# Block one of a transformer pair as a single stage: recurrence products placed between projection products, outputs token-major

## The chip, the cores and the metric

One core of one Trainium2 chip. The time is the device time of one launch in microseconds (us). The kernel before was run three times: 2466.53 us (median), 2466.32 us (lowest), 2470.12 us (highest).

## The reference

All arithmetic is float32. Block one takes 512 tokens `x` and 256 context tokens of width 1024 (8 tiles of 128 columns). Cut to what the change touches:

```
mod_x, mod_c = silu(c) @ w_ada + b_ada, silu(c_ctx) @ w_ada + b_ada   # six parts of 1024
p = modulate(rmsnorm(h), shift, scale) @ w_in      # 512 q,k | 512 v | 512 g | 32 r | 512 pool
gk_f, gk_b = log_sigmoid(r_f @ w_gk_f + b) / 16, log_sigmoid(r_b @ w_gk_b + b) / 16
# chunks of 64 positions, 4 heads, 64 keys x 128 values, forward and backward
u     = einsum(k * exp(b_last - bcum), v);  S[n+1] = exp(b_last) * S[n] + u[n]
a     = tril(einsum(q * exp(bcum - b_mid), k * exp(b_mid - bcum)))
o     = a @ v + (q * exp(bcum)) @ S[n]             # summed over both directions
mix   = concat(o * rsqrt(mean(o*o) + eps) * w_norm * silu(g),
               pool_project(window means of pool_in over 2,4,8,16 minus the token))
h     = x + g1 * (mix @ w_out)
```

The context's chunks only advance the state; they have no outputs. Then come a mixture of experts (32 experts, 4 for each token) and a second block. Neither is touched.

## The kernel before, in words

The kernel writes the order of work of each engine by hand; engines wait for each other through semaphores. Block one is five phases, each a block of its own, so that an engine begins a phase only when all engines have finished the one before.

- **phase_in (L147).** The sync engine loads `x`, the context, and then weight tiles of 2 MB into a ring of six slots in the order of `Weights` (L76 to L85): four tiles of `w_ada`, then parts of `w_in` and the other eight tiles of `w_ada`. TensorE makes modulation rows (`ada`, L260), spreads them (L271, L274), turns the tokens feature-major (L281) and makes 20 projection products (`project`, L297): 18 with 512 moving columns and two with 256, eight matmuls each. Four banks rotate; odd products are copied out by ScalarE (L231), even ones by VectorE (L417, L419). GpSimd issues 15 transfers of zeros for the experts' output (L249). The pooled features come last.
- **phase_gates (L491).** TensorE makes the gate inputs (L527); ScalarE takes them out and makes Abs, Exp and Ln (L537 to L542); VectorE takes the minimum, scales, scans four rows of 768 and subtracts (L565, L566, L569, L574, L579); ScalarE exponentiates (L545 to L553); VectorE multiplies with q and k (L584 to L589). q is spread over zeroed 128-row tiles `qmid` and `qcum`, so a score or an output of one head contracts over 128 rows of which 64 are zero. GpSimd makes window sums of two of four pooling groups (L765 to L781).
- **phase_gla (L592).** 24 transposes of the decayed keys (L632), 11 steps of the recurrence (L643 on TensorE, four updates on VectorE at L705), scores for four token tiles (L654) masked by VectorE (L714, L718), then outputs head by head and feature-major (L663, L668; 16 and 64 matmuls), their squares (L688), means over 128 features by a matmul with a tile of 1/128 (L677), a square root and a reciprocal over 2048 columns (L690, L725), norm and gate (L728, L730). GpSimd makes the other two pooling groups.
- **phase_pool (L784).** Four products with `w_pool` (L794), scaled (L801).
- **phase_out (L805).** `x` is read again (L817), 8 products with `w_out` (L826), gated and added (L840, L842).

Then the routing phase of the experts begins with its DMAs (L997, L1017) and squares (L1021).

Of the kernel before, what the change touches and what calls it, by code (L numbers as in the profile page):

```python
# [21 lines left out]
P = 128  # L22
# [29 lines left out]
ADA_FIRST = (0, 2, 1, 3)  # L52
ADA_REST = [("ada2", [6, 7]), ("ada3", [8, 9]), ("ada4", [4, 5, 10, 11])]
# [4 lines left out]
class Weights:  # L58


    def __init__(self, nc, top, k, a):
# [12 lines left out]
        ada = lambda tiles: cols(a["w_ada"], [(i * 512, 512) for i in tiles])  # L74
        win = lambda name: cols(a["w_in"], [W_IN[name]])
        add("ada1", *ada(ADA_FIRST))  # L76
        add("in_r", *win("r"))
        add("in_qk", *win("qk"))
        add("in_v", *win("v"))
        add(ADA_REST[0][0], *ada(ADA_REST[0][1]))  # L80
        add("in_g", *win("g"))
        add(ADA_REST[1][0], *ada(ADA_REST[1][1]))
        add("in_pool", *win("pool"))
        add(ADA_REST[2][0], *ada(ADA_REST[2][1]))
        add("out", *cols(a["w_out"], [(0, 512), (512, 512)]))  # L85
        self.before_moe = len(self.jobs)
# [5 lines left out]
        self.slot = [n % SLOTS if n < self.first["out2"] else (n - self.first["out2"]) % SLOTS for n in range(len(self.jobs))]  # L92
# [54 lines left out]
def phase_in(nc, k, a, w, xt, hT, g):  # L147

    ps = k.ps
    ADA1, R, QK, V, G, PL = (w.first[n] for n in ("ada1", "in_r", "in_qk", "in_v", "in_g", "in_pool"))  # L150
    columns = list(ADA_FIRST)
    tiles = [ADA1 + i for i in range(4)]
    for name, cols in ADA_REST:
        tiles += [w.first[name] + i for i in range(len(cols))]
        columns += cols
    with ExitStack() as st:
        sem = lambda n: k.semaphore(n)
        sb = lambda n, s, d=F32: st.enter_context(nc.sbuf_tensor(n, s, d))
        rows, rows2 = sb("vec_rows", [2 * KD, P]), sb("vec_rows_2", [P, P])
        brows, bcol = sb("b_ada_rows", [48, P]), sb("b_ada_cols", [P, 48])  # L160
        bg = sb("b_ada_gates", [P, 2, D])
        sig = sb("sigmoid_c", [P, 2 * KD])
        narrow = sb("silu_narrow", [P, KD, 32])
        modr = sb("mod_rows", [P, 2, P])
        pick = sb("pick_row", [P, 4, P])
        junk, ms, rt = sb("sq_junk", [P, D]), sb("ms", [P, NT]), sb("rt", [P, NT])
        zero = sb("y_zero", [P, D])
        c_in, vec_in, vec_in_2, bg_in, const_in = (sem(n) for n in ("c_in", "vec_in", "vec_in_2", "bg_in", "const_in"))
        x_in = [sem(f"x_in_{i}") for i in range(NT)]
        c_turn, c_cols, sig_done, narrow_done, v_turn, v_cols, v_zero = (sem(n) for n in ("c_turn", "c_cols", "sig_done", "narrow_done", "v_turn", "v_cols", "v_zero"))  # L170
        sq, msd, sd, xnd, x_turn, x_out, vch, modx = (sem(n) for n in ("sq", "mean_sq", "sd", "xn_done", "x_turn", "x_out", "vch", "modulated"))
        mm, rowd, picked, turn, cold, halfd = (sem(n) for n in ("ada_mm", "ada_rows", "pick_ready", "ada_turn", "ada_cols", "mod_half"))
        r_mm, r_out, pj, ev_v, ev_a = (sem(n) for n in ("r_mm", "r_out", "proj_mm", "proj_ev_v", "proj_ev_a"))
        zd, zero_out = sem("y_zero"), sem("y_zero_out")
        block = st.enter_context(nc.Block())

        jobs = []

        def feat(n, col, dst, lo, nn, post=None):
            jobs.append((n, lambda kk: w.tile(n)[:, kk, col:col + P], lambda kk: hT[:, kk, lo:lo + nn], nn, dst, post))  # L180

        for m in range(2):
            feat(QK, m * P, g.qT[:, m, :], 0, T, 64.0 ** -0.5)
        for m in range(2):
            feat(QK, 256 + m * P, g.kT[:, m, 0:T], 0, T)
            feat(QK, 256 + m * P, g.kT[:, m, T:TC], T, CTX)
        for i in range(NT):
            jobs.append((V, lambda kk, i=i: hT[:, kk, i * P:(i + 1) * P], lambda kk: w.tile(V)[:, kk, :], 512, g.v[:, i, :], None))
        for m in range(4):
            feat(G, m * P, g.gT[:, m, :], 0, T)  # L190
        for m in range(4):
            feat(PL, m * P, g.poolT[:, m, :], 0, T)

        def gate(t):
            return columns[t] // 2 in (2, 5)

        @block.sync
        def _(sp):
            for i in range(NT):
                src = a["x"][0, i * P:(i + 1) * P, :] if i < TT else a["ctx"][0, (i - TT) * P:(i - TT + 1) * P, :]  # L200
                sp.dma_start(xt[i], src).then_inc(x_in[i], 16)
            w.load(sp, 0, w.before_moe)

        @block.scalar
        def _(act):
            for name, r in VEC_LIST[0:2]:
                act.dma_start(rows[VEC[name]:VEC[name] + r, :], a["vec_views"][name]).then_inc(c_in, 16)
# [6 lines left out]
            act.dma_start(k.ones128[:], a["const_ones128"]).then_inc(const_in, 16)  # L214
            for i in range(NT):
                act.wait_ge(x_in[i], 16)
                act.activation(junk[:], xt[i], ACT.Square, accum_out=ms[:, i:i + 1]).then_inc(sq, 1)
                act.wait_ge(sq, i + 1)
            act.wait_ge(msd, 1)
            act.activation(rt[:], ms[:], ACT.Sqrt).then_inc(sd, 1)  # L220
            for i in range(NT):
                for h in range(2):
                    act.wait_ge(x_turn, 2 * i + h + 1)
                    act.activation(hT[:, 4 * h:4 * h + 4, i * P:(i + 1) * P], ps[2 * (i % 2) + h][:].rearrange("p (q t) -> p q t", q=4), ACT.Copy).then_inc(x_out, 1)
            for i, gi in enumerate((2, 5)):
                act.dma_start(bg[:, i, :], a["b_ada"][0:1, gi * D:(gi + 1) * D].to_broadcast([P, D])).then_inc(bg_in, 16)
            act.wait_ge(const_in, 16)
            for j in range(1, len(jobs), 2):
                n, lhs, rhs, nn, dst, post = jobs[j]
                act.wait_ge(pj, j + 1)  # L230
                act.activation(dst, ps[j % 4][:, 0:nn], ACT.Copy, scale=1.0 if post is None else post).then_inc(ev_a, 1)  # L231

        @block.gpsimd
        def _(pool):
            for name, r in VEC_LIST[3::2]:
                pool.dma_start(rows2[VEC[name]:VEC[name] + r, :], a["vec_views"][name]).then_inc(vec_in_2, 16)
            pool.memset(pick[:], 0.0).then_inc(picked, 1)
            for q in range(4):
                pool.wait_ge(picked, q + 1)
                pool.memset(pick[32 * q:32 * q + 1, q, :], 1.0).then_inc(picked, 1)  # L240
            pool.wait_ge(picked, 5)
            pool.memset(zero[:], 0.0).then_inc(zd, 1)
            pool.wait_ge(zd, 1)

            pool.wait_ge(pj, 6)
            first = 2 * E_ * SUB
            n = (MAX_SUBS * SUB - first) // P
            for i in range(n):
                pool.dma_start(k.y[first + i * P:first + (i + 1) * P, :], zero[:]).then_inc(zero_out, 16)  # L249
            pool.wait_ge(zero_out, 16 * n)  # L250

        @block.tensor
        def _(pe):
            def ada(t):
                w.wait(pe, tiles[t])
                if t >= 2:
                    pe.wait_ge(rowd, t - 1)
                for kk in range(KD):
                    for q in range(4):
                        last = pe.matmul(ps[4 + t % 2][32 * q:32 * q + 32, 0:P], narrow[:, kk, :], w.tile(tiles[t])[:, kk, q * P:(q + 1) * P], start=kk == 0, stop=kk == KD - 1)  # L260
                last.then_inc(mm, 1)

            def spread(t):
                pe.wait_ge(rowd, t + 1)
                if t >= 2:
                    pe.wait_ge(cold, t - 1)
                bank = ps[6 + t % 2]
                if gate(t):
                    pe.wait_ge(picked, 5)
                    for q in range(4):  # L270
                        last = pe.matmul(bank[:, q * P:(q + 1) * P], pick[:, q, :], modr[:, t % 2, :], start=True, stop=True)  # L271
# [4 lines left out]
            def turn_x(i):  # L276
# [3 lines left out]
                for kk in range(KD):  # L280
                    last = pe.transpose(ps[2 * (i % 2) + kk // 4][:, (kk % 4) * P:(kk % 4 + 1) * P], xt[i][:, kk * P:(kk + 1) * P], k.ident[:])  # L281
# [3 lines left out]
            def used():  # L285
                pe.sem_inc(w.used, 1)

            def project(lo, hi):
                for j in range(lo, hi):
                    n, lhs, rhs, nn, dst, post = jobs[j]  # L290
                    w.wait(pe, n)
                    if j >= 4:
                        pe.wait_ge(ev_v if j % 2 == 0 else ev_a, (j - 4) // 2 + 1)
                    for kk in range(KD):
                        if j == 0:
                            pe.wait_ge(modx, 2 * kk + 2)
                        last = pe.matmul(ps[j % 4][:, 0:nn], lhs(kk), rhs(kk), start=kk == 0, stop=kk == KD - 1)  # L297
                    last.then_inc(pj, 1)
# [24 lines left out]
            pe.wait_ge(mm, 4)  # L323
            for _ in range(4):
                used()

            project(0, 1)
            w.wait(pe, R)
            pe.wait_ge(rowd, 4)
            for kk in range(KD):  # L330
                for q in range(4):
                    last = pe.matmul(ps[4][32 * q:32 * q + 32, 0:192], w.tile(R)[:, kk, :], hT[:, kk, 192 * q:192 * q + 192], start=kk == 0, stop=kk == KD - 1)
            last.then_inc(r_mm, 1)
            pe.wait_ge(r_mm, 1)
            used()
            project(1, 6)
            pe.wait_ge(pj, 6)
            used()
# [2396 lines left out]
```

## Time and profile before

| what | value |
|---|---|
| time, median of 3 runs | 2466.53 us |
| time of the profiled execution | 2470.89 us |
| its span, first to last instruction | 2469.1 us |
| PE (matmul) busy | 2075.9 us, 84% |
| PEld (weight load) busy | 1019.4 us, 41% |
| VectorE (DVE) busy | 731.5 us, 30% |
| ScalarE (ACT) busy | 301.4 us, 12% |
| GpSimd (POOL) busy | 261.8 us, 11% |
| HBM traffic over the span | 221 GB/s |
| mean granted TensorE clock | 0.906 of 2.4 GHz |

PE is TensorE's matmuls, PEld its weight loads, which overlap them. A busy share says that an engine had an instruction in flight, not that it bounds the time. PEclk is the granted clock as a share of 2.4 GHz: 1.00 is 2.4 GHz and 0.50 is 1.2 GHz. "Idle before" names how long an engine stood still before a group and which instruction released it. A float32 matmul has two records in the trace, a transpose one. Block one ends some 439 us into the span.

### The profile page before, as it was taken

To read this page: it belongs to the slowest core of one execution; us is meant where nothing else is said; L and a number is where in the kernel's file an instruction comes from. 1 tells how busy PE (TensorE), PEld (TensorE's weight loads), DVE (VectorE), ACT (ScalarE), POOL (GpSimd) and SP (SyncE) were. 2 spreads that over 40 slices of the span, in tenths; PEclk is the share of its full clock that TensorE was granted. 3 is DMA by queue.
4 is the path that set the end of the run, shared out by engine and by line. 5 is a ranking of instruction groups with operands and counts; after the bars stand their busy time and mean duration, and the time that the engine had idled before them with its cause. 6 is when DMAs were issued, how large, how long until landed. Compare 5 with 4: busy or idle time off the path is not lost. (4 is left out here: it accounts for less than half of the span.)

```text
span 2469.1 us, 41438 instructions
## 1 busy us (share of the span) xinstructions
PE 2075.9 (84%) x17351; PEld 1019.4 (41%) x17351; DVE 731.5 (30%) x1338; ACT 301.4 (12%) x567; POOL 261.8 (11%) x299
## 2 busy tenths in 40 slices
PE   6992368449987989999989895199998789999998
PEld 3442263314422434433424332144776444444443
DVE  2004742413322223222323221665645320110001
ACT  2002200300000000000000000233233110000001
POOL 1105420021100111111101011100320000000000
PEclk9997659679988999999989998599997899999999
DMA  9533000669999999999999999310101311222000
GB/s 369 206 137 126 3 0 34 262 255 410 414 419 419 417 419 419 417 418 418 418 419 418 415 417 376 129 35 0 36 23 35 145 68 68 98 72 77 34 0 34
DMA packets 132029, 548.44 MB, mean 222 GB/s; under 512 B 19610, under 2 KB 32942, under 8 KB 82514
## 3 DMA queue, kind: packets, MB, share of 16 engines
q1 hardware_dynamic: 105936, 506.21, 50.9%
q0 software_dynamic: 9264, 27.04, 2.9%
q10 hardware_dynamic: 16690, 13.06, 1.7%
q8 instruction: 120, 1.97, 0.3%
q14 instruction: 19, 0.16, 0.0%
HBM read 523.54 MB, written 22.71 MB: 221 GB/s over the span
## 5 line engine op out<-in xcount | busy, mean ns | idle before, releaser
L1244 PE MATMUL ps<-W,x_modulated 128*32 128x512 f32 x3168 | 381.7, 622 | 92.6 <-DVE x_modulated L1322 43.2
L1244 PE MATMUL ps<-W_high,x_modulated 128*32 128x512 f32 x2016 | 241.2, 617 | 26.2 <-DMA W_high<-in_w_gu 20.2
L1244 PEld LDWEIGHTS ps<-W,x_modulated 128*32 128x32 f32 x3168 | 107.9, 112 | 328.0 <-issue 189.8
L2624 PE MATMUL ps<-hT,W 128*128 128x512 f32 x512 | 224.3, 599 | 3.2 <-PE ps L2624 1.8
L2662 PE MATMUL ps<-W,hid 128*128 128x512 f32 x512 | 221.6, 593 | 2.7 <-PEq L2606 1.7
L1331 DVE TENSOR_SCALAR gate<-ps 128x256 f32<-128x256 f32 x81 | 34.4, 425 | 601.8 <-PE ps L1248 601.8
L1260 PE MATMUL ps<-W,hidden_turned 128*32 128x256 f32 x3200 | 186.4, 384 | 1.1 <-DVE hidden_turned L1342 1.1
L2624 PEld LDWEIGHTS ps<-hT,W 128*128 128x128 f32 x512 | 97.6, 192 | 129.5 <-issue 129.5
L2662 PEld LDWEIGHTS ps<-W,hid 128*128 128x128 f32 x512 | 96.6, 190 | 127.7 <-issue 127.7
L1260 PEld LDWEIGHTS ps<-W,hidden_turned 128*32 128x32 f32 x3200 | 118.3, 112 | 73.9 <-issue 21.8
L1642 PE MATMUL ps<-hT,W 128*128 128x512 f32 x336 | 146.5, 594 | 2.4 <-PEq L1437 2.1
L1244 PEld LDWEIGHTS ps<-W_high,x_modulated 128*32 128x32 f32 x2016 | 71.2, 111 | 170.4 <-issue 121.6
L1285 ACT ACTIVATE sig<-gate 128x256 f32<-128x256 f32 x81 | 33.8, 418 | 693.5 <-DVE gate L1331 693.5
L1260 PE MATMUL ps<-W_high,hidden_turned 128*32 128x256 f32 x1984 | 114.1, 381 | 0.0
L1215 POOL COPY rows_idx<-slot_rows 128x1 int32 (+1 forms) x82 | 22.7, 277 | 831.2 <-DVE x_turned L1318 825.9
L1642 PEld LDWEIGHTS ps<-hT,W 128*128 128x128 f32 x336 | 63.3, 190 | 82.2 <-issue 82.0
L297 PE MATMUL ps<-hT,W 128*128 128x512 f32 (+1 forms) x224 | 93.4, 577 | 2.2 <-DMA W<-in_w_in 2.0
L1260 PEld LDWEIGHTS ps<-W_high,hidden_turned 128*32 128x32 f32 x1984 | 70.0, 111 | 46.6 <-issue 11.9
L1218 POOL DMA_INDIRECT x_rows<-moe_xn,rows_idx x82 | 80.4, 981 | 64.6 <-POOL rows_idx L1215 64.6
L2642 DVE TENSOR_TENSOR hid<-relu_tmp 128x512 f32<-128x512 f32 x32 | 22.2, 693 | 205.9 <-ACT relu_tmp L2636 205.9
L2562 PE MATMUL ps<-W,mixT 128*128 128x512 f32 x128 | 57.4, 607 | 14.0 <-PEq L1997 13.9
L1342 DVE STREAM_TRANSPOSE hidden_turned<-hidden 128x256 f32<-128x256 f32 x81 | 36.1, 446 | 110.0 <-ACT y_rows L1292 110.0
(541 smaller groups left out, 2036.0 us busy)
## 6 DMA issues: line engine op xcount, KB each, us to landing
W<-in_w_gu SPq DMA_DIRECT2D x152, 1024.0 KB, 25.4
W_high<-in_w_gu SPq DMA_DIRECT2D x104, 1024.0 KB
W<-in_w_down SPq DMA_DIRECT2D x80, 1024.0 KB, 23.5
W_high<-in_w_down SPq DMA_DIRECT2D x48, 1024.0 KB
W<-in_mlp_w SPq DMA_DIRECT2D x16, 2048.0 KB, 7.8
W<-in_w_ada SPq DMA_DIRECT2D x12, 2048.0 KB, 15.4
W<-in_w_in SPq DMA_DIRECT2D x10, 2048.0 KB, 16.8
moe_y<-y_rows ACTq DMA_DIRECT2D x324, 32.0 KB, 5.9
```

The costliest lines, as they stand in the source:

```text
L297: last = pe.matmul(ps[j % 4][:, 0:nn], lhs(kk), rhs(kk), start=kk == 0, stop=kk == KD - 1)
L1215: pool.tensor_copy(rows_idx[:], m.idx4[:, bass.ds(u, 1)]).then_inc(idx_set, 1)
L1218: pool.indirect_dma_start(xg[:], None, m.xn, bass.IndirectOffsetOnAxis(ap=rows_idx[:, 0:1], axis=0)).then_inc(x_in, 16)
L1244: last = pe.matmul(gu_out(j), xs[:, kk, :], quarter(ex.view(n), j), start=kk == 0, stop=False)
L1260: last = pe.matmul(down_bank[SUB * j:SUB * (j + 1), 0:256], hT[:, kk, :], ex.view(n)[:, kk % 2, j * 256:(j + 1) * 256], start=kk == 0, sto ...
L1285: act.activation(sig[:], gate[:], ACT.Sigmoid, scale=1.702).then_inc(sigd, 1)
L1331: dve.tensor_scalar(gate[:], gu_bank[:, 0:256], SWIGLU_LIMIT, None, ALU.min).then_inc(gated, 1)
L1342: dve.transpose(hT[:].rearrange("p k t -> p (k t)"), hid[:]).then_inc(h_ready, 1)
L1642: last = pe.matmul(ps[j % 4][:, 0:nn], lhs(kk), rhs(kk), start=kk == 0, stop=kk == KD - 1)
L2562: last = pe.matmul(ps[2 * i + half][:], mixT[:, kk, i * P:(i + 1) * P], w.tile(O2 + half)[:, kk, :], start=kk == 0, stop=kk == KD - 1)
L2624: last = pe.matmul(ps[j % 8][:], w.tile(n)[:, kk, (j % 4) * P:(j % 4 + 1) * P], hT[:, kk, :], start=kk == 0, stop=kk == KD - 1)
L2662: last = pe.matmul(ps[2 * i + half][:], hid[:, 4 * g + q, i * P:(i + 1) * P], w.tile(L + g)[:, q, half * 512:(half + 1) * 512], start=g == ...
```

## The change

The five phases become one, `phase_first`. The rest of the kernel keeps its work; the second block's weights keep their slots.

- **Projections.** The pooled features come first, then k, q, v and g; v and g in token tiles. Two banks rotate in place of four. Pooled features are copied out by VectorE; k, q and v by ScalarE, in order with its exponentials.
- **Gates.** Made after two projection products. The division by 16 moves into the scale of the exponentials, so one pass over 3072 columns goes. Eight of the bias additions go to VectorE. The scaled minimum is made for 768 columns at a time, with a wait for each.
- **Keys, recurrence, scores.** Transposes and recurrence steps stand between v products; the last seven steps and the scores stand inside the four g products. Scores contract over 64 rows (no zeroed `qmid`, `qcum`).
- **Outputs.** Token-major: for one token tile 4 matmuls with 128 rows and 16 with 64 rows, 128 moving columns. The mean of squares comes from ScalarE's accumulator in place of a product; the gate is `silu(g) * w_norm` made by VectorE and GpSimd ahead of time. Each finished tile is transposed back and goes into `out`. Output products go tile by tile, both halves of a tile together.
- **GpSimd.** The pooling groups each wait for their own eviction. Then it zeroes the state and mask tiles, which lie in the same memory. The 15 transfers of zeros go to the sync engine's queue, in pieces of 1 KB in place of 4 KB.
- **Loads.** Weight tiles have fixed homes; a load waits for the product that frees its home. The reload of `x` waits for the last output.

TensorE's order after the opening (which stays):

```diff
+            pe.wait_ge(pool_in, 16)
+            project(0)
+            ...  (the r product)
+            project(1)
+            gates(0)
+            project(2)
+            gates(1)
+            ada(4)
+            project(3)
+            spread(4)
+            project(4)
+            ada(5)
+            project(5)
+            project(6)
+            spread(5)
+            ada(6)
+            project(7)
+            project(8)
+            spread(6)
+            ada(7)
+            project(9)
+            spread(7)
+            project(10)
+            project(11)
+            pe.wait_ge(feat, 2)
+            turn_k(0)
+            turn_k(1)
+            project(12)
+            pe.wait_ge(kdone, 2)
+            update(0)
+            project(13)
+            update(1)
+            turn_k(2)
+            turn_k(3)
+            project(14)
+            update(2)
+            project(15)
+            update(3)
+            turn_k(4)
+            turn_k(5)
+            ada(8)
+            for i in range(TT):
+                project(PROJ_G + i, 0, 3)
+                update(4 + 2 * i if i < 3 else 10)
+                project(PROJ_G + i, 3, 6)
+                if i < 3:
+                    update(5 + 2 * i)
+                scores(i)
+                project(PROJ_G + i, 6, KD)
+                spread(8 + i)
+                if i < 3:
+                    ada(9 + i)
+            pooled(0); pooled(1); outputs(0); pooled(2); pooled(3); outputs(1)
+            turn_mix(0); outputs(2); turn_mix(1); outputs(3)
+            out(0); turn_mix(2); out(1); turn_mix(3); out(2); out(3)
```

The rule by which a product waits for its bank, and ScalarE's order around the exponentials:

```diff
+            def project(j, lo=0, hi=KD):
+                    if 2 <= j < 6:
+                        pe.wait_ge(ev_v, j - 1)
+                    elif 6 <= j < 18:
+                        pe.wait_ge(ev_a, j - 5)
+                    elif j >= 18:
+                        pe.wait_ge(gmul, j - 17)
...
+            evict(4, k_out[0])
+            evict(5, k_out[1])
+            act.wait_ge(dl, 4)
+            act.activation(el, el, ACT.Exp, scale=1.0 / 16.0).then_inc(ee, 1)
+            evict(6, k_out[2])
+            act.wait_ge(dm, 4)
+            act.activation(ei, em, ACT.Exp, scale=-1.0 / 16.0).then_inc(ee, 1)
+            act.wait_ge(ee, 2)
+            act.activation(em, em, ACT.Exp, scale=1.0 / 16.0).then_inc(ee, 1)
+            evict(7, k_out[3])
```

The sync engine's order after the first four `w_ada` tiles:

```diff
+            sp.dma_start(w_r[:], ...); sp.dma_start(w_pool_in, ...); sp.dma_start(inv, ...); sp.dma_start(wp[:], ...)
+            sp.wait_ge(mm, 1)
+            load(0, w_ada(4))
+            sp.wait_ge(mm, 2)
+            load(1, w_cols(a["w_in"], *W_IN["qk"]))
+            ...  (v in two halves)
+            sp.wait_ge(mm, 3)
+            load(2, w_cols(a["w_in"], *W_IN["g"]))
+            for t in range(5, 9):
+                sp.wait_ge(mm, t)
+                load(0, w_ada(t))
+            for i in range(fills):
+                sp.dma_start(k.y[...].rearrange("p (q n) -> p q n", q=4), zero[...].to_broadcast([P, 4, 256])).then_inc(zero_out, 16)
+            sp.wait_ge(pj, PROJ_V)
+            load(1, w_cols(a["w_out"], 0, 512))
+            for t in range(9, 12):
+                sp.wait_ge(mm, t)
+                load(0, w_ada(t))
+                ...  (its bias row, after cold t)
+            sp.wait_ge(pj, PROJ_END)
+            load(2, w_cols(a["w_out"], 512, 512))
+            sp.wait_ge(o, TT)
+            ...  (x again, four transfers)
```

`mm` counts `ada` products, `pj` projections, `ev_v` and `ev_a` evictions by VectorE and ScalarE, `dl` and `dm` the subtractions, `feat` the products with q and k, `o` the outputs.

## Rows read from the trace of the kernel before

**Rows 1.** Busy time by stretch: us, busy by engine, granted clock, DMA share, GB/s.

```profile
42.10:204.60 162.50, 157.06 (x932) 81.32 (x932) 13.99 (x33) 5.55 (x10) 7.94 (x15) 0.98 0.57 211
204.60:278.00 73.40, 2.95 (x33) 2.47 (x33) 46.47 (x31) 25.77 (x28) 31.10 (x20) 0.55 0.09 31
278.00:313.90 35.90, 25.10 (x264) 20.02 (x264) 24.71 (x59) 6.78 (x8) 34.29 (x23) 0.79 0.02 5
313.90:348.10 34.20, 34.16 (x160) 34.16 (x161) 4.48 (x1) 1.79 (x3) 8.20 (x4) 0.50 0.00 0
348.10:382.10 34.00, 10.81 (x19) 4.04 (x18) 24.23 (x17) 3.79 (x3) 0.00 (x0) 0.65 0.00 0
382.10:437.70 55.60, 55.41 (x128) 24.12 (x128) 9.70 (x15) 0.00 (x0) 0.00 (x0) 1.00 0.11 38
```

**Rows 2.** TensorE in order of time: start, us, line, operation, idle before.

```profile
42.16 9.84 PE L297 MATMUL ps<-hT,W 128*128 128x512 f32 x16 [2.02 <-DMA W<-in_w_in]
51.92 2.81 PE L332 MATMUL ps<-hT,W 128*32 128x192 f32 x64
...
124.70 3.70 PE L260 MATMUL ps<-W,silu_narrow 128*32 128x128 f32 x128 [0.30 <-PE ps L297]
...
203.43 1.16 PE L271 MATMUL ps<-mod_rows,pick_row 128*128 128x128 f32 x8 [0.41 <-DVE mod_rows L381]
215.09 2.94 PE L527 MATMUL ps<-rT,wgk 32*128 32x192 f32 x32 [10.50 <-DMA wgk<-in_w_gk_b]
278.00 5.42 PE L632 MATMUL ps<-ident,elast 128*128 128x128 f32 x24 [59.96 <-PEq L497]
...
287.35 0.69 PE L643 MATMUL ps<-h,cum 64*64 64x128 f32 x16 [0.54 <-DVE S_ctx L705]
...
302.10 2.05 PE L654 MATMUL ps<-W 128*128 128x128 f32 x16 [1.52 <-DVE a_masked L714]
...
313.94 0.80 PE L663 MATMUL ps<-elast,h 128*128 128x128 f32 x2 [2.81 <-DVE elast L718]
...
375.55 5.25 PE L794 MATMUL ps<-poolT,w_pool_sb 128*128 128x512 f32 x8 [21.87 <-PEq L597]
...
409.95 27.70 PE L826 MATMUL ps<-W,mixT 128*128 128x512 f32 x64
```

**Rows 3.** ScalarE in order of time, in the gates stage and the opening.

```profile
9.37 0.19 ACT L217 ACTIVATION_READ_ACCUMULATOR sq_junk<-h 128x1 f32 x1
...
221.95 2.76 ACT L540 ACTIVATE W<-W 128x3072 f32<-128x3072 f32 x1
...
230.10 2.76 ACT L542 ACTIVATE W<-W 128x3072 f32<-128x3072 f32 x1
```

**Rows 4.** VectorE in order of time, the gates stage, the recurrence, the end.

```profile
232.97 3.94 DVE L565 SCALAR_TENSOR_TENSOR W<-W 128x3072 f32<-128x3072 f32 x1 [17.22 <-ACT W L542]
...
250.13 3.57 DVE L574 TENSOR_TENSOR elast<-cum 128x768 f32<-128x768 f32 x4
...
289.85 8.47 DVE L705 SCALAR_TENSOR_TENSOR W<-W,decay,ps 128x128 f32<-128x128 f32 x28
...
438.42 0.69 DVE L842 TENSOR_TENSOR h<-h,W 128x512 f32<-128x512 f32 x1
```

**Rows 5.** The scans' line: durations in ns, least, median, most.

```profile
L569 DVE TENSOR_TENSOR_SCAN cum<-scan_mask,W x4: 1726/2212/2748, 241.4 to 248.4; 128x768 f32<-128x768 f32 x4
```

**Rows 6.** GpSimd in order of time: transfers of zeros, additions of the second and third pooling group.

```profile
83.27 7.94 POOL L249 DMA_DIRECT2D moe_y<-y_zero  x15 [73.51 <-PE ps L297]
...
233.77 6.01 POOL L777 TENSOR_TENSOR pool_rows<-mixT 128x1344 f32<-128x1344 f32 x1
...
288.73 3.08 POOL L777 TENSOR_TENSOR pool_rows<-mixT 128x1344 f32<-128x1344 f32 x1
```

**Rows 7.** PE by stretch: us, busy, granted clock, DMA share, GB/s.

```profile
111.00:118.00 7.00, 7.00 (x18) 1.00 0.00 0
```

More of the change, by code:

```diff
@@ new lines, in phase_first, with state @@
+        tile = lambda i: slice(i * P, (i + 1) * P)
+        o_bank = lambda i: 6 if i % 2 == 0 else 4
+        out_bank = lambda i: 0 if i % 2 == 0 else 6
+        def state(d, step):
+            n = order[d][step] if step < NCH else None
+            if n is None or n >= XCH:
+                return S_ctx[:, step % 2, 2 * d:2 * d + 2, :]
+            return S[:, n, 2 * d:2 * d + 2, :]
+        jobs = [(lambda kk, m=m: w_pool_in[:, kk, tile(m)], lambda kk: hT[:, kk, 0:T], T) for m in range(4)]
@@ L240, in _ @@
                 pool.memset(pick[32 * q:32 * q + 1, q, :], 1.0).then_inc(picked, 1)
+            link = linker(pool, pch)
             pool.wait_ge(picked, 5)
[L242 to L249, printed above, removed]
@@ L270, in spread @@
                     for q in range(4):
-                        last = pe.matmul(bank[:, q * P:(q + 1) * P], pick[:, q, :], modr[:, t % 2, :], start=True, stop=True)
+                        last = pe.matmul(bank[:, tile(q)], pick[:, q, :], modr[:, t % 2, :], start=True, stop=True)
                     last.then_inc(turn, 1)
@@ new lines, in gates, with turn_k @@
+            def gates(d):
+                if d:
+                    pe.wait_ge(z_a, 1)
+                for m in range(2):
+                    for q in range(4):
+                        r = slice(32 * q, 32 * q + 32)
+                        last = pe.matmul(ps[4 + q][:, m * 192:m * 192 + 192], wgk[r, d, tile(m)], rT[r, :], start=True, stop=True)
+                last.then_inc(gk_mm, 1)
+            def turn_k(n):
+                i = STATE_TILES[n]
+                if n >= 2:
+                    pe.wait_ge(kdone, n - 1)
+                for q in range(4):
+                    last = pe.transpose(ps[4 + n % 2][:, tile(q)], el[:, q, tile(i)], k.ident[:])
+                last.then_inc(tr, 1)
@@ new lines, in update @@
+            def update(step):
+                if step:
+                    pe.wait_ge(sdone, 4 * step)
+                for d in range(2):
+                    n = order[d][step]
+                    r = halfs[n % 2]
+                    for h in range(4):
+                        at = (h // 2) * P
+                        last = pe.matmul(ps[6 + d][halfs[h % 2], at:at + P], el[r, 2 * d + h // 2, (n // 2) * P + 64 * (h % 2):(n // 2) * P + 64 * (h % 2) + 64],
+                                         v[r, n // 2, h * P:(h + 1) * P], start=True, stop=True)
+                last.then_inc(u, 1)
@@ L294, in project, with out @@
+            def out(i):
+                pe.wait_ge(mev, i + 1)
+                if i == 1:
+                    pe.wait_ge(mixed, 3)
+                for half in range(2):
+                    if i == 0:
+                        pe.wait_ge(slot_in[1 + half], 48)
+                    if i >= 2:
+                        pe.wait_ge(oev, 2 * (i - 2) + half + 1)
                     for kk in range(KD):
-                        if j == 0:
-                            pe.wait_ge(modx, 2 * kk + 2)
-                        last = pe.matmul(ps[j % 4][:, 0:nn], lhs(kk), rhs(kk), start=kk == 0, stop=kk == KD - 1)
@@ L298, in project @@
-                    last.then_inc(pj, 1)
+                        last = pe.matmul(ps[out_bank(i) + half][:], mixT[:, kk, tile(i)], slot[1 + half][:, kk, :], start=kk == 0, stop=kk == KD - 1)
+                    last.then_inc(omm, 1)
             pe.wait_ge(c_in, 48)
@@ L322, in _ @@
             spread(3)
[L323 to L329, printed above, removed]
+            pe.wait_ge(pool_in, 16)
+            project(0)
+            pe.wait_ge(r_in, 16)
             for kk in range(KD):
                 for q in range(4):
-                    last = pe.matmul(ps[4][32 * q:32 * q + 32, 0:192], w.tile(R)[:, kk, :], hT[:, kk, 192 * q:192 * q + 192], start=kk == 0, stop=kk == KD - 1)
+                    last = pe.matmul(ps[3][32 * q:32 * q + 32, 0:192], w_r[:, kk, :], hT[:, kk, 192 * q:192 * q + 192], start=kk == 0, stop=kk == KD - 1)
@@ L373, in _ @@
+            out(3)
         @block.vector
@@ L581, in _ @@
+            col(5)
+            row(6)
+            col(6)
+            dve.wait_ge(ev_a, 4)
             dve.wait_ge(ee, 6)
@@ new lines, in _ @@
+            dve.wait_ge(zeroed, 2)
+            dve.wait_ge(const_in, 32)
+            for step in range(4):
+                advance(step)
+            row(8)
+            for i in range(TT):
+                advance(4 + 2 * i if i < 3 else 10)
+                if i < 3:
+                    advance(5 + 2 * i)
+                mask(i)
+                gated(i)
+                col(8 + i)
+                if i < 3:
+                    row(9 + i)
+            dve.wait_ge(halfd, 4)
+            dve.wait_ge(cold, 12)
```

860 lines of the change are left out of this document (374 added, 486 removed).

## The prediction

> **What bounds the kernel now.** I read the busy time by stretch first. Up to 204.6 us TensorE works nearly without a gap at full clock; in the next 73.4 us it works 2.95 us, then 25.1 of 35.9, then 34.2 us at a granted clock of 0.50, then 10.8 of 34.0; the output projection fills 55.6 us at 1.00 [rows 1]. So from 204.6 to 382.1 us, 177.5 us, block one is a chain of elementwise stages with small matmuls between. The order of time shows why: TensorE stands 60.0 us for the gates phase to end and 21.9 us for the norm [rows 2]. Nothing is in flight to hide it, for each phase waits for all engines. DMA is idle too (shares 0.00 to 0.09), so no transfer bounds this part [rows 1]. The experts start after block one in both kernels; what block one saves, the kernel saves.
>
> **The sum, in TensorE's order.** The sum is made against the profiled execution (span 2469.1 us, own time 2470.9 us, 4.4 us over the median of the runs), in which block one's last VectorE instruction ends at 439.1 us [rows 4].
>
> *Opening.* Same work to 42.2 us, where the first projection waits for the fifth 2 MB tile [rows 2]; the pool columns take its place in the queue, behind the same bytes. Unchanged.
>
> *Projections and modulation, kept.* The first product took 9.84 us because the clock had to rise; 8 half products of the output projection took 27.7 us at full clock counted as four of 16 records each, 6.9 us a product [rows 2]. So 9.8 + 17 x 6.9 = 127.1, two of 256 columns at half of that 6.9, the r product 2.8, eight `ada` at 3.70 / 2 = 14.8, four spreads of a gate row at 1.16 and four single transposes at about 0.2: 5.4. Together 157.0 us.
>
> *Moved in.* Gate inputs: 2.94 us at a clock near 0.55, half of that at full clock; I take 1.5 (ends 1.5 and 2.9). Transposes of keys: 5.4 us at a low clock; I take 3.3 (ends 2.7 and 5.4). Eleven steps at 0.69 us: 7.6. Scores: 2.05 us a tile now, with 128 rows; the 64-row form is not in the trace. It has half the rows per matmul and the same columns, and is nearest to the recurrence row, 16 records of 64 rows in 0.69; I take 1.5 each, 6.0 (ends 2.8 and 8.2) [rows 1, 2]. Sum 18.4, and TensorE's dense part would end at 42.2 + 157.0 + 18.4 = 217.6 us.
>
> *Does the gate chain stay under the projections?* Gate inputs stand at about 70 us. Bias additions end near 73; Abs to the end of Ln took 10.9 us [rows 3]: 83.8. On VectorE a minimum over 3072 columns took 3.94, a scan 1.73 to 2.75, the subtraction 3.57 for four [rows 4, 5]. The short scans ran with GpSimd idle, the long ones beside its pooling, and a GpSimd addition that takes 3.08 alone took 6.01 there [rows 6]: the two slow each other. Now the whole chain runs beside pooling, so I take 1.0 to 1.2 for a minimum of 768, 2.5 for a scan and 5.4 for the subtractions: 83.8 + 4 x 3.8 + 0.3 + 5.4 = 104.8. ScalarE then exponentiates 3072 columns (2.8), and only behind that copies product 6 out: 108.2. Product 8 needs that bank and would be ready at 103.8. **Here is the wait that the change adds: 4.4 us**, ends 0 and 12. Queued behind it on ScalarE are the other exponentials and the copy of product 7, done by 113, before product 9 needs it at 115. The keys' feature multiply ends near 121 to 125, and the transposes need it at 139: covered by two v products, 13.8 us.
>
> The Trainium skill, page "SBUF — State Buffer", section on how the engines reach it, says that a VectorE instruction with two SBUF inputs and a GpSimd one that reads SBUF exclude each other, the later one blocking fully. By it each of some 16 VectorE instructions could wait out a whole GpSimd addition. The rows show a slowing of both, up to double, which agrees in kind; the rival below prices it.
>
> *Pooling.* GpSimd is busy 31.1 + 34.3 + 8.2 = 73.6 us with the four groups, slow stretches included [rows 1]. From 62.4 us, where the second group's input is out (the first group fits ahead of it), 65 us of work remain; with slowing it ends by 127 to 138, zeroing 2.4 us more. The first recurrence step is due at 147 and the second, which needs VectorE's answer, at 154. Hidden, with 13 us to spare; if that cover goes, every us over is paid by TensorE.
>
> *Recurrence.* A step needs four VectorE updates, 28 in 8.47 us, so 1.2 us [rows 4]; the pieces of a projection between two steps are 2.6 us or more. Hidden, and so are masks (about 2.7 us a tile) within the 12 us of one g turn.
>
> *Loads.* `w_ada` tiles 5 to 7 are issued when the previous one is used and needed 8 us or more later; a tile of 2 MB takes 5.2 us at some 400 GB/s. Tile 9 is issued near 178 and needed near 189. Hidden.
>
> *Dense part ends at* 217.6 + 4.4 + 1.5 for a clock that may fall in that wait = 223.5 us.
>
> *Tail.* Two pooling products (0.9 to 1.3 each), outputs of tile 0, two more, outputs of tile 1. A tile's outputs are 8 records at about 0.2 to 0.4 and 32 records of 64 rows at 0.69 for 16: 2.5 to 4 us [rows 2]; now all took 34.2 us at half clock. Then ScalarE squares four heads (with accumulator reads at 0.19, about 1.8 us) [rows 3], VectorE and ScalarE exchange mean, root and reciprocal (about 1), four multiplies at 0.3. A tile's chain is some 5 us and overlaps the next tile's outputs, but tiles 0 and 1 must be normed before outputs 2 and 3, which stand ahead of `out`. By this count `out` starts 17.5 us after the dense part (ends 14 and 23): 241.0 us.
>
> *Output projection.* 8 x 6.9 = 55.4 and two turns of 0.55, and 1.5 for the clock: 299.4. The second half of `w_out`, issued near 222 and landing near 229, is in time. The last tile's gating and additions are three VectorE instructions of 0.7 in place of two: block one ends at about 301.6 against 439.1.
>
> The saving is 137.5 us, rounded to 138. Against the median, 2466.5 - 138 = 2328.5; I write **2328 us**.
>
> The outputs run at a granted clock of 0.50 now though TensorE never pauses [rows 1]. The Trainium skill, page "TensorE: Matmul & The Clock Gate", Part 1, says that the low state is the default and sustained activity lifts it. That row speaks against it as busy time reads it: 34 us of back-to-back records kept 1.2 GHz. By the rule the tail would be the 14 us end of my range, by the row nearer to 23.
>
> **The rivals.**
> *VectorE and GpSimd block each other.* For: 6.01 against 3.08, 2.75 against 1.73. Against: over that stretch VectorE lost only about a third. If each of 16 instructions loses 1.5 us, the subtractions are done 24 us later than alone, some 17 later than I count, and pooling slips past 154: TensorE stands about 20 us more. 2348 us.
> *The clock falls in the dense part.* For: 0.79 in the stretch of recurrence and scores. Against: 0.98 with `ada` and spreads between the products. Falling at six places costs 3 us each, as the first product's 9.84 shows against 6.9, and low-clock outputs 6 more: about 24 us, 2352 us.
> *Slower than before: the zeros block the sync queue.* 15 transfers of 512 KB, 7.9 MB in 1 KB pieces now stand ahead of `w_out` and tiles 9 to 11 of `w_ada`. Issued near 117, they may take until 184 unseen. To eat 138 us as well they would have to take over 205 us, under 38 GB/s. With 4 KB pieces they and a weight tile were all in within 28 us: issued from 83.3, DMA share 0.00 from 111 [rows 6, 7]. A fourfold cost would be 112 us and 45 us lost (2373), sevenfold makes the kernel slower, about 2475.
> *Everything hides*, with no wait at product 8 and a short tail: 2315.
>
> **How the numbers follow.** Forecast 0.58, blocking 0.17, clock 0.13, all hidden 0.08, zeros costly 0.04, of which half ends slower. The range 2312 to 2354 takes in the bounds above and both slow rivals. What a measurement tells from no change is 0.2%, 5 us; no case ends near it. Faster 0.97, same 0.01, slower 0.02.
>
> **What would show it.** Right: TensorE's dense stretch from 42 us ends at 218 to 228, one wait of several us before product 8 released by ScalarE, none at the first recurrence steps, `out` starting near 241 and 56 us long, experts starting near 302. Wrong: a wait for GpSimd's zeroing, a wait for a DMA before an `ada` or `out`, a clock under 0.9 between 60 and 220 us, or an expert stage whose own length changes.

## The result and the profile after

The median of the runs is 2333.16 us (2330.41 to 2334.77) against 2467.15 us before (2466.32 to 2470.12): ratio 0.9461, interval 0.9449 to 0.9472. The change makes the kernel 134.0 us faster. The prediction said 2328 us, range 2312 to 2354, 0.97 for faster: right, and 5 us too low.

Busy time by stretch, after (columns as in [rows 1]):

```profile
42.20:83.00 40.80, 40.77 (x236) 19.72 (x237) 6.09 (x15) 13.29 (x13) 31.72 (x25) 0.96 0.74 273
83.00:137.00 54.00, 39.94 (x283) 23.03 (x282) 47.45 (x29) 13.02 (x14) 44.23 (x21) 0.91 0.41 139
137.00:233.20 96.20, 96.17 (x712) 50.85 (x710) 29.86 (x76) 10.40 (x17) 3.86 (x3) 1.00 0.48 166
233.20:248.20 15.00, 14.17 (x177) 9.89 (x177) 8.13 (x24) 6.29 (x30) 1.27 (x1) 1.00 0.40 141
248.20:304.30 56.10, 56.08 (x140) 25.02 (x136) 10.04 (x20) 2.43 (x11) 0.00 (x0) 1.00 0.11 38
```

Where [rows 1] had four stretches, 177.5 us in all, in which TensorE mostly stood idle or ran at half clock, it now works through, but for 14 us between 83 and 137. From 137 to 233 us, where recurrence and scores stand between the pieces of projections, it has no gap and a granted clock of 1.00. The tail that took 34.2 us of outputs and 34.0 us of norm takes 15.0.

TensorE in order of time, after (start, us, line, operation, idle before), the rows that answer to [rows 2]:

```profile
42.23 8.57 PE L474 MATMUL ps<-hT,W 128*128 128x512 f32 x16 [3.95 <-DMA W<-in_w_in]
...
105.33 0.47 PE L451 MATMUL ps<-ident,mod_rows 128*128 128x128 f32 x1 [7.61 <-DVE mod_rows L684]
105.73 3.64 PE L435 MATMUL ps<-W,silu_narrow 128*32 128x128 f32 x64
...
124.45 1.95 PE L435 MATMUL ps<-W,silu_narrow 128*32 128x128 f32 x64
...
158.03 0.68 PE L504 MATMUL ps<-h,W 64*64 64x128 f32 x16
...
192.17 1.16 PE L515 MATMUL ps<-W 64*128 64x128 f32 x16
...
248.20 14.00 PE L561 MATMUL ps<-W,hT 128*128 128x512 f32 x32
```

TensorE's three largest waits from 42 to 300 us, after (line, what it waited for: us in total, times, longest):

```profile
PE ps L451 <- DVE mod_rows L684: 10.4, 3, 7.6
PE ps L474 <- DMA W<-in_w_in: 4.0, 1, 4.0
PE ps L474 <- ACT kT L332: 3.7, 2, 2.0
```

L451 turns a modulation row that VectorE has copied out of PSUM; L474 is a projection, which waits until ScalarE has copied an earlier product out. That copy stands behind ScalarE's exponentials, and these wait for VectorE's subtractions:

```profile
112.06 2.76 ACT L342 ACTIVATE W<-W 128x3072 f32<-128x3072 f32 x1 [19.49 <-DVE W L832]
...
114.73 0.58 ACT L332 ACTIVATE kT<-ps 128x512 f32<-128x512 f32 x1
```

So both wait because VectorE is late. VectorE in order of time, after, the start and the end of the gate chain:

```profile
83.19 3.97 DVE L824 SCALAR_TENSOR_TENSOR W<-W 128x768 f32<-128x768 f32 x1 [4.05 <-ACT W L328]
87.20 4.47 DVE L826 TENSOR_TENSOR_SCAN W<-state_room,W 128x768 f32<-128x768 f32 x1
91.59 3.17 DVE L824 SCALAR_TENSOR_TENSOR W<-W 128x768 f32<-128x768 f32 x1
...
105.01 0.26 DVE L684 COPY mod_rows<-ps 128x128 f32<-128x128 f32 x1
105.19 6.83 DVE L832 TENSOR_TENSOR W<-W 128x768 f32<-128x768 f32 x4
111.95 11.91 DVE L836 TENSOR_TENSOR W<-W 128x512 f32<-128x512 f32 x4
```

GpSimd over the same time (additions of the third and of the fourth pooling group, last zeroing):

```profile
83.05 10.89 POOL L411 TENSOR_TENSOR state_room<-state_room 128x1472 f32<-128x1472 f32 x3
...
111.30 12.02 POOL L411 TENSOR_TENSOR state_room<-state_room 128x1472 f32<-128x1472 f32 x4
...
126.89 1.80 POOL L418 MEMSET state_room<- 128x2048 f32 x1
```

The last two rows of VectorE and the second of GpSimd belong together: four subtractions of 512 columns last 11.91 us while four additions last 12.02 us, one for one.

Last, the sync queue, after (us in which it issued, not until the bytes landed):

```profile
126.88 24.02 SPq L275 DMA_DIRECT2D moe_y<-y_zero  x15
150.94 1.43 SPq L249 DMA_DIRECT2D W<-in_w_out  x1
```

and what the DMA engines did meanwhile (us, granted clock, DMA share, GB/s), with the median from issue to landing last:

```profile
127.00:135.00 8.00, 1.00 0.95 312
135.00:143.00 8.00, 1.00 1.09 383
143.00:151.00 8.00, 1.00 1.07 373
151.00:159.00 8.00, 1.00 0.99 329
...
moe_y<-y_zero SPq DMA_DIRECT2D x15, 512.0 KB, 8.2
```

### The profile page after: what moved, and what is told of

The parts are those of the page before. It is cut to its first block and busy times, and to the rows that moved or that the text cites. A ratio compares the mean times of both kernels' runs of the same rounds, so it can differ in the third digit from the quotient of the medians.

```text
span 2331.3 us, 41450 instructions
## 1 busy us (share of the span) xinstructions
PE 2033.8 (87%) x17359; PEld 983.8 (42%) x17359; DVE 712.5 (31%) x1352; ACT 302.7 (13%) x599; POOL 261.3 (11%) x290
## 5 line engine op out<-in xcount | busy, mean ns | idle before, releaser
L2621 PEld LDWEIGHTS ps<-hT,W 128*128 128x128 f32 x512 | 97.2, 191 | 128.7 <-issue 128.7
L474 PE MATMUL ps<-hT,W 128*128 128x512 f32 (+1 forms) x160 | 65.9, 567 | 7.6 <-DMA W<-in_w_in 4.0
L2559 PE MATMUL ps<-W,mixT 128*128 128x512 f32 x128 | 58.4, 616 | 14.0 <-PEq L1994 13.9
```

The source lines that it names most:

```text
L474: last = pe.matmul(ps[j % 2][:, 0:n], lhs(kk), rhs(kk), start=kk == 0, stop=kk == KD - 1)
L2559: last = pe.matmul(ps[2 * i + half][:], mixT[:, kk, i * P:(i + 1) * P], w.tile(O2 + half)[:, kk, :], start=kk == 0, stop=kk == KD - 1)
L2621: last = pe.matmul(ps[j % 8][:], w.tile(n)[:, kk, (j % 4) * P:(j % 4 + 1) * P], hT[:, kk, :], start=kk == 0, stop=kk == KD - 1)
```

## The experiments

Eight kernels in all; each time is a median with its range behind it, but for the last, which ran once. The changed kernel ran beside runs of the kernel before with a median of 2467.15, the first four experiments beside others (2468.52), the last four beside a third set (2466.61). A difference from the changed kernel is therefore given twice, from the medians and from the ratios; the ratios' intervals are some 3 us wide to either side. My theory: VectorE's gate chain is slowed by GpSimd's additions, all TensorE waits between 83 and 137 us are that chain, and the rest of the saving is that small matmuls no longer stand alone. Rivals: the waits come from the order of VectorE's queue alone; the saving would have come without interleaving, since the phases' waits for all engines are gone.

**no_pool_adds.** Leaves out the window additions of the third and fourth pooling group, so the pooled result of those columns is missing from the output. The line stands twice (columns and rows), and GpSimd's count of steps is lowered to match.

```diff
-                for s in range(q + 1):
+                for s in range(q + 1 if q < 2 else 0):
```

> GpSimd's window additions of the third and fourth pooling group are left out (their copies, zeroing and last two instructions stay), so the pooled features of these groups are wrong and the rest is computed as before. Theory A, VectorE and GpSimd slow each other and that stretched the gate chain: VectorE's minimum of 768 columns falls from 1.3 to 4.0 us to about 1.0, the last subtraction ends near 107 us in place of 123.8, TensorE's waits between 80 and 137 us fall from 14 us to 4 or less, and the time falls by 10 to 14 us. Rival B, the waits come from the order of the queues and the chain is slow by itself: the durations stay, and the time falls by under 2 us.

2317.85 us (2314.86 to 2320.26), ratio 0.9391 [0.9377, 0.9406]: 15.3 us less than the changed kernel by the medians, 17.3 by the ratios. VectorE in order of time:

```profile
85.75 0.96 DVE L824 SCALAR_TENSOR_TENSOR W<-W 128x768 f32<-128x768 f32 x1 [4.05 <-ACT W L328]
...
99.16 3.55 DVE L832 TENSOR_TENSOR W<-W 128x768 f32<-128x768 f32 x4
102.63 2.49 DVE L836 TENSOR_TENSOR W<-W 128x512 f32<-128x512 f32 x4
```

and TensorE's stretch:

```profile
83.00:137.00 54.00, 53.88 (x328) 29.45 (x327) 30.61 (x32) 17.06 (x17) 12.60 (x10) 1.00 0.63 218
```

The chain takes 19.4 us (85.75 to 105.1) in place of 40.7 (83.2 to 123.9), and TensorE's gap is gone with the fall of its clock. So the additions beside it cost VectorE 21.3 us. What they cost TensorE is 14.1 us of waits and 1.7 of a modulation block at half clock (3.64 against 1.95 us), 15.8 together. The two profiled executions differ by 12.8 us only, since the first projection began 1.1 us later in this one and took 10.02 us against 8.57; over the six kernels here that are the same up to there it took 8.57 to 10.18.

**row_alone.** Copies modulation row 5 out behind the first scan, ahead of the second minimum, and nothing else.

```diff
                 dve.tensor_tensor_scan(cum[:, i, back], ...)
+                if i == 0:
+                    row(5)
-            row(5)
```

> Only VectorE's copy of the modulation row of ada 5 is moved ahead of the scans, which ends TensorE's first and longest wait (7.6 us). If the waits are one chain, TensorE then waits as much longer for ScalarE's copy of product 6, product 8 starts at 115 us as now, and the time stays within 2 us. If each wait stands for itself, the time falls by 7 to 8 us, and 2 us more for the clock that fell in the wait.

2332.63 us (2329.83 to 2336.11), ratio 0.946 [0.9445, 0.9475]: no change. TensorE's waits:

```profile
PE ps L474 <- ACT kT L332: 12.9, 2, 12.0
PE ps L474 <- DMA W<-in_w_in: 3.2, 1, 3.2
PE ps L451 <- DVE mod_rows L684: 1.1, 1, 1.1
```

10.4 and 3.7 us became 1.1 and 12.9: the same 14 us, now at the next thing that hangs on the chain. The largest wait in a view was not the one to take away.

**reorder.** The chain keeps its length; what others wait for is taken out from behind it, on VectorE (rows 5 to 7 and columns 5 and 6 between the chain's steps) and on ScalarE (copies of products 6 and 7 ahead of all exponentials, of the queries ahead of all but the first).

```diff
             dve.wait_ge(cum_done, 4)
+            col(5)
+            row(6)
             for i in range(4):
...
+            col(6)
             for i in range(4):
+                if i == 2:
+                    row(7)
                 midp = 31 if i < 2 else 32
...
-            act.wait_ge(dl, 4)
-            act.activation(el, el, ACT.Exp, scale=1.0 / 16.0).then_inc(ee, 1)
             evict(6, k_out[2])
+            evict(7, k_out[3])
+            act.wait_ge(dl, 4)
+            act.activation(el, el, ACT.Exp, scale=1.0 / 16.0).then_inc(ee, 1)
+            for m in range(2):
+                evict(PROJ_Q + m, qT[:, m, :], 64.0 ** -0.5)
```

> Nothing is left out; work that does not need the gate chain is taken from behind it: the rows and columns of ada 5 to 7 stand between the scans and subtractions on VectorE, the copies of products 6 to 9 ahead of the exponentials on ScalarE. Theory B, the chain reaches TensorE only through what is queued behind it: GpSimd's and VectorE's durations stay as long as now (subtractions end near 122 us), TensorE's waits between 80 and 137 us fall from 14 us to 2 or less, and the time falls by 12 to 15 us against the changed kernel. Rival A, the length of the chain itself reaches TensorE: half of the 14 us or more comes back as a wait before the key transposes.

2321.24 us (2320.0 to 2322.53), ratio 0.941 [0.9397, 0.9423]: 11.9 us less by the medians, 12.6 by the ratios. VectorE's and TensorE's rows:

```profile
85.75 4.02 DVE L824 SCALAR_TENSOR_TENSOR W<-W 128x768 f32<-128x768 f32 x1 [4.05 <-ACT W L328]
...
114.75 3.08 DVE L702 SCALAR_TENSOR_TENSOR modc<-modc,vec 128x8 f32<-128x8 f32 x1
117.76 4.11 DVE L842 TENSOR_TENSOR W<-W 128x512 f32<-128x512 f32 x2
```

```profile
83.00:137.00 54.00, 53.56 (x325) 28.93 (x324) 44.85 (x25) 16.90 (x16) 46.76 (x24) 1.00 0.64 221
```

The chain is as slow as in the changed kernel and ends at 126.6, yet TensorE works 53.6 of 54 us. The loss came from the chain's length together with what stood behind it: taking away either one removes it.

**serial_scan.** Recurrence steps 5 to 11 and the scores stand behind the last projection instead of between its pieces; VectorE's updates and masks are moved likewise.

```diff
-                project(PROJ_G + i, 0, 3)
-                update(4 + 2 * i if i < 3 else 10)
...
+                project(PROJ_G + i)
                 spread(8 + i)
...
+            for step in range(4, NCH - 1):
+                update(step)
+            for i in range(TT):
+                scores(i)
```

> The last seven recurrence steps and all scores are taken out of the g products and stand behind them. If placing them between products is what hid them: a step then takes TensorE and VectorE about 1.2 us, a score tile 3 to 3.5 us with its masks, 8 + 13 us in all against 9 us that they cost inside the products, so the time rises by 10 to 14 us, and by up to 4 more where the clock falls. If merging the phases did all of it and the placing nothing, the time stays within 3 us.

2353.31 us (2350.79 to 2357.55), ratio 0.9536 [0.9521, 0.955]: 20.2 us more by the medians, 18.5 by the ratios, at or above the upper end of what was expected. TensorE's stretches and two rows:

```profile
227.40:240.00 12.60, 5.51 (x97) 3.57 (x96) 7.09 (x24) 0.00 (x0) 1.27 (x1) 0.74 0.48 166
240.00:254.40 14.40, 9.35 (x81) 7.92 (x81) 7.72 (x19) 0.00 (x0) 0.00 (x0) 0.50 0.01 2
```

```profile
238.34 1.15 PE L504 MATMUL ps<-h,W 64*64 64x128 f32 x16 [1.26 <-DVE state_room L722]
...
245.34 2.08 PE L515 MATMUL ps<-W 64*128 64x128 f32 x16 [1.43 <-DVE state_room L728]
```

27.0 us stand bare where the same work between projections takes 7 x 0.68 + 4 x 1.16 = 9.4 us. Of the 17.6 us between, 12.1 are waits for VectorE (7.8 and 4.3 in the waits view) and the other 5.5 are put down to the clock, at 0.50 from 240 us, which makes a step 1.15 in place of 0.68 us and a score tile 2.08 in place of 1.16. Of the 134 us, then, the interleaving of these steps is worth 18 to 20. The other 114 to 116 are what remains when only these steps are taken out again; no run parts them further, but for the clock's share in the last run below.

**pool_late.** The third pooling group waits for the chain instead of running beside it.

```diff
                 half = 1 << q
+                if q == 2:
+                    pool.wait_ge(dm, 4)
```

> Nothing is left out; GpSimd begins the third pooling group only when VectorE has made the last subtraction. Theory A, the two engines' mutual slowing stretched the gate chain: the chain ends near 101 to 104 us in place of 123.8, TensorE's waits between 80 and 137 us fall from 14 to under 3 us; GpSimd ends its zeroing near 150, just before the second recurrence step is due at 152, so the time falls by 11 to 15 us, less up to 3 for a wait there. Rival: the cover is gone and TensorE waits for the zeroing by 10 us or more, so that the time falls by under 5 us.

2321.54 us (2320.31 to 2326.66), ratio 0.9419 [0.9405, 0.9434]: 11.6 us less than the changed kernel by the medians, 10.4 by the ratios. The chain without a neighbour, and GpSimd's last zeroing:

```profile
95.90 3.55 DVE L834 TENSOR_TENSOR W<-W 128x768 f32<-128x768 f32 x4
99.37 2.49 DVE L838 TENSOR_TENSOR W<-W 128x512 f32<-128x512 f32 x4
```

```profile
149.97 1.80 POOL L420 MEMSET state_room<- 128x2048 f32 x1
```

With no work left out, parting the two engines in time brings about what the reordering does. The zeroing ends at 151.8, before the step that waits for it, so the 23 us by which it slips cost nothing. A wait of 3.5 us for a modulation row stays (3 at most were expected): VectorE's products with the keys now stand beside the moved additions and take 6.25 and 5.70 us, where they took 3.43 and 2.35 in the changed kernel.

**reorder_r_first.** The reordering, and the small product `r` (32 matmuls of 192 columns) placed ahead of the first projection, in the time in which that waits for its 2 MB tile.

```diff
-            pe.wait_ge(pool_in, 16)
-            project(0)
             pe.wait_ge(r_in, 16)
             for kk in range(KD):
+                pe.wait_ge(modx, 2 * kk + 2)
                 for q in range(4):
...
             last.then_inc(r_mm, 1)
+            pe.wait_ge(pool_in, 16)
+            project(0)
             project(1)
```

> The reordered kernel with the small r product moved ahead of the first projection product, where TensorE stands 4 us for the weight tile of the pooled columns. If that DMA wait sets the start of the dense part and the r product is hidden in it: the first projection product starts at the same 42 to 43 us, what follows it starts 2.8 us earlier, and since the clock is up earlier the product is up to 1.5 us shorter; 2.5 to 4 us less than reorder. Rival: the r product needs the last modulated feature tile, runs at half clock beside the landing tile and delays the first product by what it saves: no change.

2313.63 us (2310.54 to 2315.04), ratio 0.9384 [0.9371, 0.9397]: the fastest of all, 19.5 us below the changed kernel by the medians, 19.0 by the ratios. TensorE in order of time, first in the reordered kernel, then here:

```profile
43.33 10.02 PE L474 MATMUL ps<-hT,W 128*128 128x512 f32 x16 [4.44 <-DMA W<-in_w_in]
```

```profile
38.91 1.97 PE L592 MATMUL ps<-hT,w_r 128*32 128x192 f32 x40
...
43.15 14.00 PE L474 MATMUL ps<-hT,W 128*128 128x512 f32 x32
```

The first product starts with its tile at the same time as before (43.15 against 43.33). What is saved is the 2.8 us of `r` behind it, which now lie in the wait, and 3.0 us of clock: two products run in 14.0 us at full clock, where the first alone took 10.02. With the 0.2 us of the start that is 6.0: the gate inputs begin at 57.08 in place of 63.09 us. The medians differ by 7.6 us, the ratios, as the two ran in different sets, by 6.4. Up to 4 were expected, with 1.5 for the clock in place of 3.0.

**reorder_pool_late.** Both remedies together, on top of the kernel just shown.

> Reorder, r product first, and the third pooling group held back, together. If reorder already took all that the gate chain cost TensorE: the same time as reorder_r_first within 2 us, though the chain ends 20 us earlier. If some cost of the chain was left: 3 us or more less. A wait for the zeroing before the second recurrence step, up to 6 us, would make it slower.

2332.81 us (2330.34 to 2334.85), ratio 0.9457 [0.9443, 0.9472]: the whole gain is lost. TensorE's wait:

```profile
161.17 1.15 PE L506 MATMUL ps<-h,W 64*64 64x128 f32 x16 [15.77 <-DVE state_room L729]
```

In the reordered queue the subtractions end later (110.2 against 101.9 us), though they are as short as in pool_late: the rows and columns that were put between them wait for TensorE's modulation products.

```profile
106.76 0.17 DVE L700 TENSOR_TENSOR modc<-ps,b_ada_cols 128x8 f32<-128x8 f32 x1 [6.83 <-PE ps L453]
```

GpSimd's third group starts at 110.3, its zeroing ends at 160.0, and the second recurrence step, due near 145, stands 15.8 us. The wait was expected at up to 6 us: this is the cover of 13 us that the prediction named, used up and paid for.

**before_warm.** The kernel before, with twelve matmuls of 512 columns, whose results nobody reads, ahead of the outputs; one run.

```diff
             pe.wait_ge(sdone, 4 * (NCH - 1))
+            for _ in range(12):
+                pe.matmul(ps[6][:], t.einv[:, 0, 0:P], g.v[:, 0, :], start=True, stop=True)
```

> The kernel before with twelve products of 512 columns that nothing reads ahead of its outputs; the output's result is unchanged. They cost 10 to 11 us at full clock, up to 5 more while it rises. If the outputs ran at 0.50 of the clock because the engine had paused before them: they now run at 1.00 and take 17 us in place of 34, and the time falls by 3 us or rises by up to 1. If products of 64 moving columns behind loads of 128 weight columns don't hold the clock up: it falls back within the outputs, they take 30 us or more, and the time rises by 6 to 13 us.

2464.45 us. Busy time by stretch:

```profile
311.19:324.20 13.01, 13.01 (x24) 5.66 (x25) 4.43 (x1) 0.00 (x0) 8.18 (x4) 0.79 0.00 0
324.20:342.10 17.90, 17.90 (x162) 17.84 (x160) 0.00 (x0) 1.79 (x3) 0.00 (x0) 1.00 0.00 1
```

The same outputs that took 34.2 us at 0.50 [rows 1] take 17.9 us at 1.00, once large matmuls have raised the clock. So of the 34.2 us of outputs in the old tail 16.3 were clock and not work or waiting. In the kernel before, the clock had stood at 1.00 from 301.0 to 313.9 us; TensorE waited 2.8 us, and the outputs behind that wait ran at 0.50 [rows 1, 2]. The twelve took 13.0 of the 16.3 us themselves; one run cannot tell the small difference that is left from none.

## Why the prediction was right, point by point

*Opening* [rows 2]: right, the first projection starts at 42.23 us.

*Dense part, work*: the sum was 157.0 kept, 18.4 moved in and 1.5 of clock, 176.9 us. Measured: 191.0 us from 42.2 to 233.2 less 14.1 of waits, 176.9. That the two sums agree to a tenth is luck, for the terms inside were off both ways: the first product 8.57 us (against 9.8), gate inputs 0.93 each (1.9 against 1.5), scores 1.16 us a tile (4.6 against 6.0), steps 0.68 (7.5 against 7.6), and the clock that fell.

*The gate chain and the wait that the change adds*: here is the step that failed. "I take 1.0 to 1.2 for a minimum of 768, 2.5 for a scan and 5.4 for the subtractions ... Here is the wait that the change adds: 4.4 us, ends 0 and 12." The place was right and the size was not. The first minima took 3.97 and 3.17, the first scan 4.47, the first four subtractions 6.83. The four subtractions for the other exponent stood in the sum as done by 113 along with their exponentials; they ended at 123.9, 11.91 us for 2.49 of work. I read the slowing off a scan beside pooling, 2.75 against 1.73, and the sum of additions beside it, instead of asking what a short instruction pays behind a long one. Behind the chain I had only looked at ScalarE's copy; VectorE's own modulation row stood behind it too, and that was the first and longest wait (7.6 us). Sum 14.1 us, past the upper end of 12 that I gave, 9.7 more than taken. Signs that were named for being right are missed by it: the dense stretch ended at 233.2 us, not at 218 to 228, `out` began at 248.2, not near 241, and there was not one wait, on ScalarE, but five, the longest of them for a row of VectorE.

By the Trainium skill's page "SBUF — State Buffer", section "SBUF: two separate sides", a VectorE instruction with two SBUF inputs and a GpSimd one that reads SBUF exclude each other. The four subtractions in 11.91 us beside four additions in 12.02 agree with it one for one. I had priced the rule as a rival with 1.5 us for each of 16 instructions; the chain lost 21.3 us, 1.3 each. So the chain was slowed nearly by what the rival said (24), and by three times the 7 us that the forecast had counted. What TensorE paid for it lies between the two, 9.7 us over the forecast where the rival had about 20, and pooling, which the rival let slip past 154, was done at 128.7.

*Pooling*: hidden as forecast, done at 128.7 (127 to 138, and 2.4, was said). The runs with it held back show both sides of the cover: 151.8 costs nothing, 160.0 costs 15.8 us. *Recurrence*: hidden, no wait at any step. *Loads*: hidden.

*Tail*: 15.0 us for 17.5, near the lower end of 14. The outputs ran at full clock. On the trace of before alone the Trainium skill's page "TensorE: Matmul & The Clock Gate", Part 1, with its low state by default that sustained activity lifts, seemed contradicted by 34 us at 1.2 GHz. In the run of the warmed kernel the burst of large matmuls did bring the clock up, as the page has it; these small ones, back to back for 34 us, did not bring it up themselves, and kept 2.4 GHz for 17.9 us once it was there.

*Output projection*: 56.1 us for 58.4; the clock never fell, so the 1.5 for it wasn't paid. (The prediction's own terms, 55.4, two turns of 0.55 and 1.5, add up to 58.0, 0.4 less than it wrote.)

*Balance.* VectorE's last instruction of block one:

```profile
304.92 1.28 DVE L771 TENSOR_TENSOR h<-h,hT 128x512 f32<-128x512 f32 x2
```

It ends at 306.2 us for 301.6 forecast: 9.7 of waits, less 2.5 in the tail, 2.3 in the output projection and 0.3 at the end, is 4.6. So the mechanism that I named was the right one, its price was a third of what it cost, and the total came within 5 us because other terms were too high. Against 439.1 [rows 4] block one saved 132.9 us. The spans differ by 137.8 us, 4.9 more, in stages that the change doesn't touch. The experts kept their length (from their first weight load to their last gate row 991.2 us before, 990.5 after); 3.0 of the 4.9 come behind them, in the second block. The profiled execution of before was 4.4 us above its median, and the medians differ by 134.0. I take that for scatter of that one execution; it isn't shown further.

*Rivals.* Zeros on the sync queue: refuted. The 15 transfers were issued within 24.0 us, and the last, issued at 149.5, landed at the latest 10.3 us later: 33 us in all, where I allowed 67 and feared 112, and no `w_ada` tile was waited for. (The prediction's "sevenfold" was not worked out right: seven times 28 is 196 us, less than the 205 that it says would be needed to lose the whole gain.) Clock: fell once, in the wait, at a cost of about 1.7 us. Everything hides: not in this kernel, but it is what the reordering makes (2321), and with `r` ahead 2314.

## What to carry to other kernels

When an elementwise chain is moved beside another engine's work, list everything that stands behind it on its own queue and on the next engine's, and take those short copies out first: 12 us came from order alone, with the chain as slow as ever. A removed wait must be looked for again at the next consumer, as row_alone shows, and two remedies that each use the same slack can cancel each other. Small matmuls with a wait in each step belong between pieces of a large product, which both hides the wait and keeps TensorE's clock up.

## What was not expected of the hardware

A modulation multiply of 8 columns took 3.08 us on VectorE beside a GpSimd addition (the L702 row of the reordered kernel), and 0.17 in the changed kernel at 136.9 us, where GpSimd had ended: what a VectorE instruction pays there doesn't go by its size but by what is left of the neighbour's. Copies out of PSUM went free of it: the copy of a modulation row took 0.26 us beside the additions (at 105.01) and 0.28 without them (at 135.95). The loss is one-sided. Four GpSimd additions of 1472 columns took 12.02 us beside VectorE's subtractions and 10.4 us in the runs where VectorE was past its chain, 16% more; VectorE's four took 11.91 against 2.49, nearly five times as long.

The same small matmuls (160 records in one trace, 162 in the other) ran at a granted clock of 0.50 for 34.2 us before and at 1.00 for 17.9 us after a burst of twelve large ones. They kept a clock that they hadn't brought up.

While the zeros went out in 1 KB pieces, with a weight tile on either side of them, the DMA engines moved 312 to 383 GB/s. I had allowed 67 us for their 7.9 MB, some 120 GB/s, a third of that.
